# Six row tiles of the last product as seven block products over pairs of tiles, with the sums of w_out's blocks formed in the opening and kept in DRAM

## The chip, the core and the metric

The kernel runs on one core of a Trainium2 chip. The metric is the device time of one execution in microseconds; the median of three runs of the kernel before is 822.89 us (822.22 to 822.99). Times in the profile are counted from the start of the span.

## The reference, cut to what matters

One layer of a hybrid encoder block on x of 1024 rows by 1024 channels, float32. Everything up to `merged` stays as it is; the change touches the last product.

```python
h = rmsnorm(x, g_pre);  proj = h @ w_in
# stick-breaking attention (8 heads) and gated linear attention (4 heads), each gated and projected to 1024
merged = sigmoid(g_A) * y_sb + sigmoid(g_B) * y_gla
x = x + merged @ w_out                  # (1024 x 1024) @ (1024 x 1024): the last product
y = rmsnorm(x, g_final)
```

## The kernel before

**Products.** A float32 operand is split into a high part (type float32r, made by a copy on ScalarE) and a low part (operand minus high part, a subtraction on VectorE). A product is three passes on TensorE: high by high, high by low, low by high. One matmul takes a 128x128 stationary tile and 512 columns of the moving operand.

**Opening.** SyncE loads the rows of x and the first tiles of w_in; ScalarE and VectorE normalise the rows (`x_normed` counts tiles), TensorE turns them in rounds of four (`turn_x`), and ScalarE (`h_high`) and VectorE (`h_low`) evacuate each round as the two parts of h. TensorE interleaves the rounds with the first projection tiles (`first_tile`) and a low-rank product. ScalarE and VectorE then evacuate q, k and v halves (`stage`), split q and k of the first heads (`stack`), and SyncE copies them to the other 64 partitions (`twin`, SBUF to SBUF). The attention loop `pair` follows: in each of its steps TensorE makes scores, ScalarE takes two sigmoids of them (`sig_done`), and the scores of the next step wait for that. All DMAs of weights go out from SyncE in the order in which they are written, on one queue. POOL only sets constants here.

**Gates and the merge.** Seven gate tiles v = 0 to 6 are each computed as seven block products (`gate_block`, 12 matmuls each; `prod_done` counts them). After the last of them `merge_last` writes the last channel tile of the merged matrix, `mT[:, 0]` (channels on partitions, all 1024 rows as columns); `m_step` reaches 23 then.

**Last product** (L925 to L945). For each of eight row tiles t and both column halves e, TensorE accumulates 24 matmuls (8 channel tiles, 3 passes) into one of four PSUM banks (`ring4`). The stationary operand is the merged tile, split by `split_m` on ScalarE (L1326) and VectorE (L1837); tile 0 is split in two goes (`split_m0`, L1213 and L1741), since its last channel tile comes late. The moving operand is w_out, loaded by `load_wout` (L512) in eight chunks and split by `wout_high` and `wout_low`. The bank's order is t0 e0, t0 e1, t1 e0 and so on. VectorE adds x to each bank (`row_sum`, L1861), ScalarE sums the squares and takes the root, VectorE scales (L1875), SyncE stores. The last half row has a path of its own: L1346 (squares), L1350 (root), L1889 (reciprocal), L1891 and L1354 (scaling), L546 and L548 (stores). POOL spreads g_final over the partitions (L577).

## Time and profile before

| what | value |
|---|---|
| median of three runs | 822.89 us |
| the profiled execution's own time | 822.67 us |
| its span | 820.9 us |
| TensorE matmul busy | 799.9 us (97%) |
| VectorE busy | 551.0 us (67%) |
| ScalarE busy | 394.8 us (48%) |
| POOL busy | 10.6 us (1%) |
| DMA engines' mean busy share | 25.1% on the one large queue, 63.13 MB |

The page gives shares over the whole span; the order of work at a given place is read from the timeline, and what sets the end from the chain that ended last. The granted clock of TensorE is full in all 40 slices of the page. Matmuls overlap, so one that is listed with 389 ns occupies less than that of the chain.

### The profile page before, as it was taken

The page shows a single profiled execution, that of the slowest core. Times are in us where ns is not written, and L with a number is a line of the kernel's source. Part 1 is how long each engine was busy: PE and PEld are TensorE (multiplying, and loading weights), DVE is VectorE, ACT ScalarE, POOL GpSimd, SP SyncE. Part 2 cuts the span into 40 slices and gives each one's busy share as a digit, 9 for nine tenths or more (in the row PEclk, how much of TensorE's full clock was granted, in tenths as well). Part 3 has the DMA queues.
Part 4 walks back from the last instruction along what each step waited for, and adds up shares of the span by engine and source line. Part 5 has one row for each costly group of instructions (what it writes and reads, how often), then busy time and mean ns, then how long its engine had stood idle before and what let it go on. Part 6 is the DMA issues. An engine that isn't in the chain of part 4 may idle for free.

```text
span 820.9 us, 11756 instructions
## 1 busy us (share of the span) xinstructions
PE 799.9 (97%) x4477; PEld 669.1 (82%) x4477; DVE 551.0 (67%) x776; ACT 394.8 (48%) x679; POOL 10.6 (1%) x16
## 2 busy tenths in 40 slices
PE   5999999999999999999999999999999999999997
PEld 4778888888888888879889888888888888878885
DVE  6528896989698698946545655665467776873332
ACT  8536675756666465654254153344333333542221
POOL 1000000000000000020000000000000000010000
PEclk9999999999999999999999999999999999999999
DMA  8122011212110220121110001243433444352321
GB/s 290 54 52 52 26 40 40 49 43 59 38 39 26 52 51 26 27 78 53 52 32 21 28 27 52 89 148 131 144 104 104 121 126 127 138 206 102 103 101 54
DMA packets 69714, 63.72 MB, mean 78 GB/s; under 512 B 3724, under 2 KB 57127, under 8 KB 69672
## 3 DMA queue, kind: packets, MB, share of 16 engines
q1 hardware_dynamic: 69618, 63.13, 25.1%
q8 instruction: 29, 0.48, 0.2%
q14 instruction: 13, 0.11, 0.0%
q10 hardware_dynamic: 54, 0.01, 0.0%
HBM read 47.40 MB, written 11.53 MB: 72 GB/s over the span
## 4 chain that ended last, share of the span: by engine, by line
PE 82%; DVE 10%; issue 3%; ACT 2%; DMA 2%; DVEq 0%; SPq 0%; ACTq 0%
PE pj L611 21%; PE ob L942 5%; PE ob L863 5%; PE sc L863 5%; PE sc L942 5%; PE tr L915 4%; PE pj L755 4%; PE ob L915 4%; DVE surv L1460 4%; PE pj L627 4%; PE pj L915 4%; PE ob L703 3%; PE sc L915 3%; PE tr L713 3%; PE pj L736 3%
## 5 line engine op out<-in xcount | busy, mean ns | idle before, releaser
L611 PE MATMUL pj<-h_hi,w_lo 128*128 128x512 f32 x336 | 134.2, 399 | 0.0
L611 PE MATMUL pj<-h_hi,w_hi 128*128 128x512 f32 x336 | 133.8, 398 | 0.0
L611 PE MATMUL pj<-h_lo,w_hi 128*128 128x512 f32 x336 | 133.7, 398 | 0.0
L1460 DVE TENSOR_TENSOR_SCAN surv<-surv 128x128 f32<-128x128 f32 (+3 forms) x64 | 86.5, 1351 | 19.2 <-ACT beta L1046 18.7
L611 PEld LDWEIGHTS pj<-h_hi,w_lo 128*128 128x128 f32 x336 | 63.5, 189 | 12.1 <-issue 0.5
L611 PEld LDWEIGHTS pj<-h_lo,w_hi 128*128 128x128 f32 x336 | 63.3, 188 | 12.1 <-issue 0.3
L611 PEld LDWEIGHTS pj<-h_hi,w_hi 128*128 128x128 f32 x336 | 63.5, 189 | 11.7 <-issue 0.2
L1087 ACT ACTIVATE wt_hi<-tr 128x512 fp32r<-128x512 f32 (+2 forms) x96 | 43.6, 490 | 43.2 <-PE tr L713 41.7
L1385 DVE TENSOR_TENSOR w_lo<-w_raw,w_hi 128x1024 fp32r<-128x1024 f32 x33 | 40.3, 1222 | 26.6 <-ACT w_hi L980 26.5
L1505 DVE TENSOR_TENSOR wt_lo<-tr,wt_hi 128x512 fp32r<-128x512 f32 (+2 forms) x96 | 50.1, 549 | 5.3 <-ACT wt_hi L1087 4.8
L1463 DVE TENSOR_TENSOR beta<-beta,surv 128x128 f32<-128x128 f32 (+3 forms) x64 | 48.6, 759 | 2.2
L1045 ACT ACTIVATE surv<-sc 128x128 f32<-128x128 f32 (+3 forms) x64 | 41.8, 654 | 13.8 <-PE sc L681 13.0
L713 PE MATMUL tr<-ident,beta 128*128 128x128 f32 x288 | 43.1, 277 | 4.0 <-DVE wt_lo L1505 4.0
L1046 ACT ACTIVATE beta<-sc 128x128 f32<-128x128 f32 (+3 forms) x64 | 41.6, 651 | 0.0
L713 PEld LDWEIGHTS tr<-ident,beta 128*128 128x128 f32 x288 | 32.4, 140 | 11.1 <-DVE wt_lo L1505 5.9
L980 ACT ACTIVATE w_hi<-w_raw 128x1024 fp32r<-128x1024 f32 x33 | 34.9, 1057 | 9.7 <-PE ob L863 9.3
L703 PE MATMUL ob<-wt_hi,v_st 128*128 128x256 f32 (+1 forms) x160 | 38.0, 272 | 0.5
L703 PE MATMUL ob<-wt_lo,v_st 128*128 128x256 f32 (+1 forms) x160 | 37.6, 282 | 0.0
L679 PE MATMUL sc<-k_hi,q_st 128*128 128x512 f32 (+2 forms) x96 | 37.1, 387 | 0.0
L755 PE MATMUL pj<-vn_hi,h_hi 128*128 128x256 f32 x128 | 36.5, 285 | 0.1
L755 PE MATMUL pj<-vn_hi,h_lo 128*128 128x256 f32 x128 | 36.4, 284 | 0.0
L755 PE MATMUL pj<-vn_lo,h_hi 128*128 128x256 f32 x128 | 36.3, 284 | 0.0
(326 smaller groups left out, 1868.2 us busy)
## 6 DMA issues: line engine op xcount, KB each, us to landing
w_raw<-in_w_in SPq DMA_DIRECT2D x30, 512.0 KB, 3.8
y_scratch<-y_ring SPq DMA_DIRECT2D x28, 256.0 KB, 2.0
graw<-in_w_in SPq DMA_DIRECT2D x14, 512.0 KB, 4.7
y_back<-y_scratch SPq DMA_DIRECT2D x14, 512.0 KB, 5.2
x_t<-in_x SPq DMA_DIRECT2D x8, 512.0 KB, 6.4
wout_raw<-in_w_out SPq DMA_DIRECT2D x8, 512.0 KB, 7.0
x_res<-in_x SPq DMA_DIRECT2D x8, 512.0 KB, 3.7
out_y<-y_out SPq DMA_DIRECT2D x16, 256.0 KB, 2.2
```

The source lines that it names most:

```text
L611: mm = pe.matmul(pj[bank][:, :], (w_lo if p == 2 else w_hi)[:, slot, k, :], (h_lo if p == 1 else h_hi)[:, k, HALF * h:HALF * h + HALF], st ...
L703: mm = pe.matmul(ob[gg % 2][:, c0:256], v_st[:, e, b, :], part[g % 2][:, b, c0:256], start=(b == 0 and part is wt_hi), stop=(b == blocks - ...
L713: mm = pe.transpose(tr[n % 2][:, P * b:P * b + P], beta[:, unit % 2, P * (b0 + b):P * (b0 + b) + P], ident[:, :])
L755: mm = pe.matmul(pj[c % 2][:, 256 * (t % 2):256 * (t % 2) + 256], (h_lo if p == 2 else h_hi)[:, k, P * t:P * t + P], (vn_lo if p == 1 else ...
L863: mm = pe.matmul(ring4[c % 4], (w_lo if p == 2 else w_hi)[:, slot, 4 * side + k, :], (g_lo if p == 1 else g_hi)[:, G_SLOT[4 * br + k], HAL ...
L915: mm = pe.matmul(bank_of, (gw_lo if p == 2 else gw_hi)[j][:, k, :], moving[j][p == 1][:, k, :], start=(j < 4 and k == 0 and p == 0), stop= ...
L942: mm = pe.matmul(ring4[c % 4], (m_lo if p == 2 else m_hi)[t % 2][:, k, :], (wout_lo if p == 1 else wout_hi)[e][:, u, :], start=(u == 0 and ...
L1045: act.activation(surv[:, step % 2, 0:keys], sc[:, 0:keys], ACT.Sigmoid, scale=-HD ** -0.5)
L1087: act.activation(wt_hi[g % 2][:, b0:b0 + nb, P * (unit % 2):P * (unit % 2) + P], tr[n % 2][:, 0:P * nb].rearrange("p (b q) -> p b q", q=P) ...
L1460: dve.tensor_tensor_scan(s[:, ::-1], s[:, ::-1], s[:, ::-1], 1.0, ALU.mult, ALU.bypass)\
L1463: dve.tensor_tensor(beta[:, step % 2, 0:keys], beta[:, step % 2, 0:keys], surv[:, step % 2, 1:keys + 1], ALU.mult).then_inc(w_ready, 1)
L1505: dve.tensor_tensor(wt_lo[g % 2][:, b0:b0 + nb, qs], tr[n % 2][:, 0:P * nb].rearrange("p (b q) -> p b q", q=P), wt_hi[g % 2][:, b0:b0 + nb ...
```

## The change

Rows of x in tiles 0 and 1 are computed as before, in another order (both tiles by one column half, then both by the other). Tiles 2 to 7 are taken in three pairs p = 1, 2, 3. A pair's 256 rows by 1024 channels and w_out's 1024 by 1024 are each cut into four blocks, and the pair's result is made of seven block products (`out_block`) of 12 matmuls instead of eight. The four sums of w_out's blocks do not depend on the data: POOL forms them in the opening from w_out's rows, ScalarE and VectorE split them, and SyncE stores both parts in DRAM (`w_scratch`, eight stores of 1 MB) and reads them back (`load_tw`, eight loads of 1 MB) around the start of the last product. The sums of the merged blocks are formed by POOL per pair. VectorE puts the seven products together in nine steps (`gather`, counted by `pair_step`) on x_res, which now holds four rows of tiles; ScalarE copies one bank out per pair (`copy_u2`). y_row and y_out are gone: rows are scaled in place and stored whole, with one DMA for 512 KB, but for tile 6, the last, which is stored in halves. In the opening the eight small loads of w_up are issued later.

```diff
+        x_res = at("x_res", 8, [P, 4, D])
...
+        w_dram = nc.dram_tensor("w_scratch", (2, 4, P, 4, HALF), F32, kind="Internal").ap()
...
+            def load_wrow(k):
+
+                if k >= 2:
+                    sp.wait_ge(wsum_done, 4 * (k - 2) + 4)
+                sp.dma_start(wrow[k % 2][:, :, :], w_out_v[:, k::4, :]).then_inc(wrow_loaded[k % 2], 16)
+
+            def store_wsum(part, k):
+
+                if part == 0:
+                    sp.wait_ge(wsum_hi, 2 * k + 2)
+                else:
+                    sp.wait_ge(wsum_lo, 2 * k + 2)
+                sp.dma_start(w_dram[part, :, :, k, :].rearrange("t p c -> p t c"),
+                             (wsum_l if part else wsum_h)[k][:, :, :].bitcast(F32))\
+                    .then_inc(wsum_stored[4 if k == 3 and part else k], 16)
@@ -447,10 +489,23 @@
...
 
+            load_wrow(0)
+            load_wrow(1)
             load(3, COL_Z, 1)
             load(4, COL_Q + P, 0)
+            for c in range(8):
+                sp.dma_start(w_up[RANK * c:RANK * (c + 1), :], w_alpha_up[0]).then_inc(up_loaded, 16)
+            load_wrow(2)
+            load_wrow(3)
+            for k in range(3):
+                for part in range(2):
+                    store_wsum(part, k)
             twin(0, 2)
             load(5, COL_K + P, 1)
+            for part in range(2):
+                store_wsum(part, 3)
+            for n, stores in enumerate((32, 32, 32, 16, 16)):
+                sp.wait_ge(wsum_stored[n], stores)
@@ -525,29 +580,51 @@
...
+            def load_tw(n):
+
+                for part in range(2):
+                    sp.dma_start(tw[n][part][:, :, :].bitcast(F32), w_dram[part, n]).then_inc(tw_loaded[n], 16)
...
-                if t >= 2:
...
-                    store(t - 1)
+            sp.wait_ge(prod_done, NP * NP - 1)
+            load_tw(2)
+            sp.wait_ge(m_step, 3 * NP + 2)
+            load_res(0)
+            sp.wait_ge(prod_done, NP * NP)
+            load_tw(3)
+            sp.wait_ge(wout_l, KT)
+            load_tw(1)
+            sp.wait_ge(o5_ready, 2)
+            load_tw(0)
+            load_res(1)
@@ -561,6 +638,22 @@
...
+            pool.wait_ge(x_normed, ST)
+            for k in range(4):
+                top, low = wrow[k % 2][:, 0, :], wrow[k % 2][:, 1, :]
+                ts = wsum[k]
+                pool.wait_ge(wrow_loaded[k % 2], 16 * (k // 2) + 16)
+                if k == 2:
+                    pool.wait_ge(tr_ready, R0)
+                if k == 3:
+                    pool.wait_ge(wsum_stored[0], 32)
+                pool.tensor_tensor(ts[:, 0, :], top[:, HALF:D], top[:, 0:HALF], ALU.subtract).then_inc(wsum_done, 1)
+                pool.tensor_tensor(ts[:, 2, :], low[:, HALF:D], top[:, HALF:D], ALU.subtract).then_inc(wsum_done, 1)
+                pool.wait_ge(wsum_done, 4 * k + 1)
+                pool.tensor_tensor(ts[:, 1, :], low[:, HALF:D], ts[:, 0, :], ALU.subtract).then_inc(wsum_done, 1)
+                pool.wait_ge(wsum_done, 4 * k + 3)
+                pool.tensor_tensor(ts[:, 3, :], low[:, 0:HALF], ts[:, 1, :], ALU.subtract).then_inc(wsum_done, 1)
@@ -575,6 +668,24 @@
...
+
+            pool.wait_ge(m_ready, 2)
+            pool.wait_ge(m_step, 3 * NP + 2)
+            for p in range(1, 4):
+                a, b = slice(2 * P * p, 2 * P * p + P), slice(2 * P * p + P, 2 * P * p + 2 * P)
+                o11, o21, o12, o22 = mT[:, 4:KT, a], mT[:, 4:KT, b], mT[:, 0:4, a], mT[:, 0:4, b]
+                if p > 1:
+                    pool.wait_ge(om_low, NP * (p - 2) + 6)
+                pool.tensor_tensor(os3[:, :, :], o11, o21, ALU.subtract).then_inc(os_ready, 1)
+                pool.wait_ge(os_ready, 4 * (p - 1) + 1)
+                pool.tensor_tensor(o21, o21, o22, ALU.add).then_inc(os_ready, 1)
+                pool.wait_ge(os_ready, 4 * (p - 1) + 2)
+                if p == 1:
+                    pool.wait_ge(o5_ready, 4)
+                pool.tensor_tensor(os2[:, :, :], o21, o11, ALU.subtract).then_inc(os_ready, 1)
+                pool.wait_ge(os_ready, 4 * (p - 1) + 3)
+                pool.wait_ge(om_low, NP * (p - 1) + 1)
+                pool.tensor_tensor(o12, o12, os2[:, :, :], ALU.subtract).then_inc(os_ready, 1)
...
+            for c in range(4):
+                t, e, part = c % 2, 1 - c // 2, c // 2
+                if c == 0:
+                    pe.wait_ge(comb, 5 * (NP - 1))
+                    pe.wait_ge(sig_a, 2 * (NP - 1))
+                if c == 1:
+                    pe.wait_ge(mt_lo, 3)
...
+            READ_BY = {4: 3, 5: 2, 6: 4}
+            TW_OF = {1: 3, 3: 0, 4: 1, 5: 2}
...
+                if o in READ_BY:
+                    pe.wait_ge(pair_step, done + READ_BY[o])
+                if p == 1 and o in TW_OF:
+                    pe.wait_ge(tw_loaded[TW_OF[o]], 32)
+                pe.wait_ge(om_low, NP * (p - 1) + o + 1)
+                bank_of = gate_banks[(p + 1) % 2][OUT_BANK[o]]
+                for j in range(4):
+                    for q in range(3):
+                        mm = pe.matmul(bank_of, (om_lo if q == 2 else om_hi)[o][:, 3 - j, :],
+                                       out_moving[o][q == 1][:, j, :], start=(o < 4 and j == 0 and q == 0),
+                                       stop=(j == 3 and q == 2), skip_group_check=True)
@@ -1022,17 +1166,39 @@
...
+            def wsum_high(k, half):
+
+                hs = slice(2 * half, 2 * half + 2)
+                act.wait_ge(wsum_done, 4 * k + 4)
+                if k == 2:
+                    act.wait_ge(wsum_stored[0], 32)
+                act.activation(wsum_h[k][:, hs, :], wsum[k][:, hs, :], ACT.Copy).then_inc(wsum_hi, 1)
...
-            h_high(range(KT + 3, R0))
+            h_high([KT + 3])
+            wsum_high(0, 0)
+            h_high([KT + 4])
+            wsum_high(0, 1)
+            h_high(range(KT + 5, R0))
             stage(v_t, 2, 0, 0)
+            for half in range(2):
+                wsum_high(1, half)
             stage(stage_q, 3, 1, 1)
+            for half in range(2):
+                wsum_high(2, half)
             stage(stage_k, 4, 1, 0)
             act.wait_ge(proj_free, 5)
+            act.wait_ge(wsum_stored[1], 32)
             for part in range(2):
                 stack(0, part)
             high_part(3, 1, 2, proj_ready, 5)
+            wsum_high(3, 0)
             stage(v_t, 5, 1, 1)
+            wsum_high(3, 1)
             lr_quarters(1)
+            act.wait_ge(wsum_lo, 8)
+            act.wait_ge(wsum_stored[2], 32)
+            act.wait_ge(wsum_stored[3], 16)
 
@@ -1318,40 +1484,93 @@
...
+            def high_out(p, o):
+
+                if p == 1:
+                    if o < 3:
+                        act.wait_ge(prod_done, NP * NP)
+                        act.wait_ge(m_step, 3 * NP + 2)
+                    if o == 3:
+                        act.wait_ge(fin_bc, 1)
+                    if o >= 4:
+                        act.wait_ge(o5_ready, 4 if o == 6 else 3)
+                else:
+                    act.wait_ge(out_prod, NP * (p - 2) + o + 1)
+                if o >= 3:
+                    act.wait_ge(os_ready, 4 * (p - 1) + (2, 3, 1, 4)[o - 3])
+                act.activation(om_hi[o][:, :, :], out_source(p, o), ACT.Copy).then_inc(om_high, 1)
@@ -1437,16 +1656,37 @@
...
+            def wsum_low(k, half):
+
+                hs = slice(2 * half, 2 * half + 2)
+                dve.wait_ge(wsum_hi, 2 * k + half + 1)
+                dve.tensor_tensor(wsum_l[k][:, hs, :], wsum[k][:, hs, :], wsum_h[k][:, hs, :].bitcast(F32),
+                                  ALU.subtract).then_inc(wsum_lo, 1)
...
+            h_low(range(KT + 3, KT + 5))
+            wsum_low(0, 0)
+            h_low([KT + 5])
+            wsum_low(0, 1)
+            h_low(range(KT + 6, R0))
             stage(v_t, 2, 0, 0)
+            for half in range(2):
+                wsum_low(1, half)
             stage(stage_q, 3, 1, 1)
+            for half in range(2):
+                wsum_low(2, half)
             stage(stage_k, 4, 1, 0)
+            dve.wait_ge(wsum_stored[1], 32)
             for part in range(2):
                 stack(0, part, part)
             low_part(3, 1)
             stage(v_t, 5, 1, 1)
+            dve.wait_ge(proj_ready, 6)
+            for half in range(2):
+                wsum_low(3, half)
             lr_quarters(1)
+            dve.wait_ge(wsum_stored[2], 32)
+            dve.wait_ge(wsum_stored[3], 16)
             dve.wait_ge(const_done, 1)
@@ -1848,47 +2083,113 @@
...
+            dve.wait_ge(mt_hi, 3)
+            dve.tensor_tensor(m_lo[1][:, :, :], mT[:, :, P:2 * P], m_hi[1][:, :, :].bitcast(F32), ALU.subtract)\
+                .then_inc(mt_lo, 1)
             for c in range(5, KT):
                 wout_low(c)
+            dve.wait_ge(xr_loaded[0], 32)
+            row_sum(0)
+            for o in range(2):
+                low_out(1, o, o)
+            row_sum(1)
+            for o in range(2, 4):
+                low_out(1, o, o)
+            row_sum(2)
+            row_sum(3)
+            low_out(1, 4, 5)
+            low_out(1, 5, 4)
+            low_out(1, 6, 6)
...
+            norm_row(0, 0)
+            norm_row(1, 1)
+
+            for p in range(1, 4):
+                row, done = 2 * (p % 2), OP_STEPS * (p - 1)
+                banks = gate_banks[(p + 1) % 2]
...
+                if p > 1:
+                    norm_row(2 * p - 2, 2 * ((p - 1) % 2) + 1)
+                    norm_row(2 * p - 1, 2 * ((p - 1) % 2))
+                dve.wait_ge(xr_loaded[p % 2], 32 * (p // 2 + 1))
+                gather(1, 1, xa1, banks[0], xa1, ALU.add, 0)
+                gather(2, 2, xb2, xb2, banks[3], ALU.subtract, 0)
+                next_low(0)
+                next_low(1)
+                gather(3, 3, xa1, banks[1], xa1, ALU.add, 1)
+                next_low(2)
...
+                next_low(3)
+                dve.wait_ge(u2_copied, p)
+                gather(5, 5, xa2, o_sum[:, :], xa2, ALU.add, 0)
+                next_low(4)
+                gather(6, 6, o_sum[:, :], o_sum[:, :], banks[3], ALU.add, 5)
+                gather(6, 7, xb1, xb1, o_sum[:, :], ALU.add, 6)
+                gather(6, 8, xb2, xb2, o_sum[:, :], ALU.add, 6)
+                next_low(5)
+                gather(7, 9, xa2, banks[2], xa2, ALU.add, 5)
+                next_low(6)
+
+            dve.wait_ge(ss5, 15)
+            dve.wait_ge(y_done, 5)
+            dve.reciprocal(stats[:, 52:53], stats[:, 50:51]).then_inc(rstd5, 1)
+            dve.wait_ge(rstd5, ST - 1)
+            dve.scalar_tensor_tensor(out=x_res[:, 3, :], in0=x_res[:, 3, :], scalar=stats[:, 52:53], in1=g_fin[:, :],
+                                     op0=ALU.mult, op1=ALU.mult).then_inc(y_done, 1)
+            dve.wait_ge(ss5, 17)
+            dve.wait_ge(y_done, 6)
```

## Rows read from the trace of the kernel before

**Rows 1.** The page, section 1: busy time by engine (share of span, instructions).

```profile
PE 799.9 (97%) x4477; PEld 669.1 (82%) x4477; DVE 551.0 (67%) x776; ACT 394.8 (48%) x679; POOL 10.6 (1%) x16
```

**Rows 2.** Chain that ended last, last product: start us, us, what.

```profile
732.37 6.41 PE sc L942 x27
...
749.66 10.88 PE sc L942 x48
```

**Rows 3.** The same chain in the opening.

```profile
59.15 3.05 PE pj L611 x13
62.19 0.12 PE sc L679
```

**Rows 4.** Timeline of ScalarE, opening: start us, us, engine, line, operation, tiles, shapes.

```profile
50.68 1.06 ACT L991 ACTIVATE q_st<-stage_q 64x1024 fp32r<-64x1024 f32 x1 [0.49 <-DVE stage_k L1399]
...
59.33 1.28 ACT L1040 ACT_TABLE_LOAD   x1
...
60.89 0.27 ACT L1046 ACTIVATE beta<-sc 128x128 f32<-128x128 f32 x1
```

**Rows 5.** Timeline of VectorE, opening: the last row tile normalised.

```profile
24.80 0.75 DVE L1380 TENSOR_SCALAR x_t<-x_t,stats 128x1024 f32<-128x1024 f32 x1
```

**Rows 6.** Timeline of SyncE's queue: the first twin copy and the loads behind it.

```profile
54.27 0.54 SPq L439 DMA_DIRECT2D k_hi<-k_hi  x1
...
55.49 12.57 SPq L423 DMA_DIRECT2D w_raw<-in_w_in  x2
```

**Rows 7.** Windows: length, engines' busy time, PEclk, DMA share, GB/s at the end.

```profile
55.50:56.00 0.50, 0.50 (x4) 0.25 (x3) 0.34 (x1) 0.13 (x1) 0.00 (x0) 1.00 0.99 221
...
59.50:60.00 0.50, 0.50 (x4) 0.41 (x3) 0.26 (x1) 0.50 (x1) 0.00 (x0) 1.00 0.44 129
...
819.00:819.50 0.50, 0.00 (x0) 0.00 (x0) 0.00 (x0) 0.00 (x0) 0.00 (x0) 1.00 1.02 389
```

**Rows 8.** Timeline of POOL over the whole span.

```profile
14.58 0.28 POOL L559 TENSOR_SCALAR_AFFINE_SELECT ident_bf<-ident_bf 128x128 bf16<-128x128 bf16 x1 [11.68 <-issue]
...
361.28 0.68 POOL L570 TENSOR_SCALAR_AFFINE_SELECT mask<-mask 128x512 f32<-128x512 f32 x1
362.02 1.58 POOL L573 TENSOR_SCALAR_AFFINE_SELECT mask<-mask 64x512 f32<-64x512 f32 x1
...
726.92 2.23 POOL L577 PARTITION_BROADCAST g_fin<-g_fin_row  x1 [363.25 <-DMA g_fin_row<-in_g_final]
```

**Rows 9.** Timeline of ScalarE around and in the last product.

```profile
697.72 0.63 ACT L1254 ACTIVATE gw_hi<-graw 128x512 fp32r<-128x512 f32 x1 [5.08 <-DMA graw<-in_w_in]
...
731.68 0.31 ACT L1213 ACTIVATE m_hi<-mT 128x128 fp32r<-128x128 f32 x1 [2.35 <-DVE mT L1846]
731.90 2.00 ACT L1205 ACTIVATE wout_hi<-wout_raw 128x1024 fp32r<-128x1024 f32 x2
...
750.43 1.06 ACT L1335 ACTIVATE junk<-y_row 128x1024 f32<-128x1024 f32 x1 [7.17 <-DVE y_row L1861]
```

**Rows 10.** Timeline of VectorE around and in the last product.

```profile
728.49 1.06 DVE L1844 TENSOR_TENSOR gates<-gates,y_back 128x512 f32<-128x512 f32 x1
...
730.19 0.69 DVE L1844 TENSOR_TENSOR gates<-gates,y_back 128x512 f32<-128x512 f32 x1
...
732.02 0.29 DVE L1741 TENSOR_TENSOR m_lo<-mT,m_hi 128x128 fp32r<-128x128 f32 x1 [0.42 <-ACT m_hi L1213]
732.23 3.49 DVE L1749 TENSOR_TENSOR wout_lo<-wout_raw,wout_hi 128x1024 fp32r<-128x1024 f32 x3
735.64 1.22 DVE L1837 TENSOR_TENSOR m_lo<-mT,m_hi 128x1024 fp32r<-128x1024 f32 x1
...
742.53 1.42 DVE L1875 SCALAR_TENSOR_TENSOR y_out<-y_row,stats,g_fin 128x512 f32<-128x512 f32 x2
```

**Rows 11.** Timeline of all engines, the tail.

```profile
816.85 0.17 DVE L1889 RECIPROCAL stats<-stats 128x1 f32<-128x1 f32 x1 [1.18 <-ACT stats L1350]
...
818.17 0.43 SPq L548 DMA_DIRECT2D out_y<-y_out  x1
```

267 lines of the change are left out of this document (169 added, 98 removed).

## Prediction

> **What bounds the kernel now.** I read the engine line of the page first: TensorE is busy 97% of the span and no other engine over 67% [rows 1]. So an edit gains only if it takes matmuls away, and costs only where it makes TensorE wait. Next, the chain that ended last, for the last product: 48 matmuls, two banks, take 10.88 us [rows 2], so one costs 10.88/48 = 0.2267 us. In that chain all is TensorE but one gap: at 732.37 us it resumes with 27 matmuls, three of the first bank and 24 of the second. It had waited for the last channel tile of row tile 0, whose parts come from ScalarE at 731.68 and VectorE at 732.02 [rows 9, 10]. Last, the opening, in which the change puts a second stage of work: TensorE makes the scores of step 0, runs 13 projection matmuls from 59.15, and at 62.19 makes the scores of step 1 [rows 3]. These need step 0's sigmoids, which end at 60.89 + 0.27 = 61.16 [rows 4]. That is 1.0 us of slack, and it is where I expect the main cost.
>
> **What is removed.** Before, 16 banks of 24 are 384 matmuls. After, 4 banks of 24 and 3 pairs of 7 products of 12 are 96 + 252 = 348. 36 fewer at 0.2267 us is **-8.16 us**. Each of the new products is on TensorE's path back to back, in the same three-pass form, so I take the same pace.
>
> **The sums of w_out in the opening.** POOL may start when the last row tile is normalised, 24.80 + 0.75 = 25.55 [rows 5]. It makes four operations of 128x512 for each of four k, 16 in all. No row shows a two-input operation on POOL. The nearest are a selection of the same shape at 0.68 us and one on 64 partitions at 1.58 us [rows 8]; I take the middle, 1.13, and 1.2 from start to start with the semaphore. The Trainium skill (GPSIMD Engine Reference, Performance versus the Vector engine) gives 4497 ns for a float32 tensor_tensor of 2048 elements; a quarter is an estimate of 1.12 us, and the sum would be the same by it.
>
> k = 0 is then done at 30.4 and k = 1 at 35.2. ScalarE takes the first of them behind a round of h at about 32.3 and TensorE needs the rounds behind it only from about 41, so these ten copies and subtractions lie in idle time of both engines. What does not is SyncE's queue, since one DMA is served after the other. From k = 1 on it holds the load of rows k = 3 and six stores, 1 MB each. Stores run at 389 GB/s in the tail with the DMA engines full [rows 7]; with a little less, 380, one takes 2.76 us. The first is issued at 35.2 and starts 1.1 us later, as the twin copy issued at 54.27 does, which has the engines full by 55.5 [rows 6, 7]. So 36.3 + 7 x 2.76 = 55.6: the queue is never empty, and k = 1's stores land just at about 50.5, when ScalarE and VectorE, who now wait for them, would split q and k at 50.68 [rows 4]. The twin copies and the load of w_raw behind them hold the engines from about 55.3 to 59.8 before, 4.5 us [rows 6, 7]; now from 55.6 to 60.1. The store of k = 3's high parts is issued at about 56.7 (ScalarE copies them after the v half) and comes behind: 60.1 + 2.76, and 0.4 until its semaphore, 63.3. ScalarE and VectorE wait for exactly this store before the loop. Behind ScalarE's wait are a table load of 1.28 us and the first sigmoids, 61.16 - 59.33 = 1.83 us in all [rows 4]: 65.1 against the 62.19 at which TensorE needs them. The stall is **+3.0 us**. Its ends: if the store did not queue behind the copies it would land at 56.7 + 1.1 + 2.76 + 0.4 = 61.0 and the stall be 0.6; if a POOL operation takes 1.58, everything behind the eighth moves by 8 x 0.45 = 3.6 us, 6.6 in all. Afterwards nothing is given back, since TensorE is full from there.
>
> **The order of tiles 0 and 1.** Bank 1 is now tile 1, not tile 0, and waits for the whole low part of tile 1. ScalarE makes the high part after tile 0's last piece, at 731.90, in about 1.04 us (it did two of 1024 in 2.00), and VectorE the low part in 1.22 [rows 9, 10]: 731.90 + 1.04 + 0.04 + 1.22 = 734.20. TensorE ends bank 0 at 732.37 + 3 x 0.2267 = 733.05. **+1.2 us**; before, this work had a whole bank as cover. POOL now starts its first sum of the merged tiles at the same event as tile 0's last piece. The one row with POOL and VectorE busy together is a multiplication of 128x512 at 728.49, which takes 1.06 us under the broadcast that starts at 726.92 for 2.23; the same at 730.19 takes 0.69 [rows 8, 10]. I add this 0.37 once: **+1.6 us** in all. Ends 1.2 and 3.3 (the lock, below).
>
> **The first pair.** Its fifth product reads into a bank that VectorE must have gathered (step 3). Count from the end of bank 3. VectorE adds bank 3 (0.7), ScalarE sums and roots the row (1.5, from 1.06 and two small ones), copies a sum's high part (0.6), VectorE makes three low parts (1.85 at 0.6 from start to start), scales two rows (a reciprocal of 0.17 and 1.42 each, 3.2), gathers twice and makes two low parts (2.4), and gathers step 3 (0.7): 11.0 us [rows 9 to 11]. TensorE comes there after 48 matmuls, 10.88. So 0.1 to 0.3 us, and with 0.4 for POOL, which forms the second pair's sums in just this stretch, **+0.7 us**; ends 0.2 and 2.5. In pair 2 no row adds and fewer low parts come ahead of step 3, 8.4 against 10.9: covered. The loads of the sums are 8 MB. The last that the first pair needs early (fourth product, about 759) is issued at 739.7 behind about 4 MB, 11 us at 389 GB/s: on chip at about 753, covered by 6 us.
>
> **The tail.** The last half row's path is the same, but VectorE has a whole row to scale (1.42) and its reciprocal (0.17) between, after the row's root, about 0.9 us after TensorE ends. It is free at 2.5 us, while before the last reciprocal came 1.9 us after the end [rows 10, 11]: +0.6. That row's store of 512 KB is ahead of the last two, 1.35 us of the queue, most of it over before the last is issued 3.8 us after TensorE's end: +0.3. **+0.9 us**, ends 0.6 and 1.3. The x loads and stores of the pairs have over 5 us each.
>
> **The sum.** -8.16 + 3.0 + 1.6 + 0.7 + 0.9 = -1.96 us. The profiled execution takes 822.67 us, 0.2 under the median of 822.89; the same difference on the median gives 820.9 us.
>
> **Rivals.** (1) *The opening is nearly free*: the store of k = 3 does not queue behind the copies, stall 0.6, and the sum is -4.4, 818.5 us. For it: the copies between partitions move only 221 GB/s with the engines at 0.99 [rows 7], so something may run beside them. Against: the same 0.99. (2) *POOL is slow*, and the forecast turns to slower: the price is 8 times what an operation takes over 1.2 us from start to start. At 0.45 us more, the 1.58 of the row, the sum is -1.96 + 3.6 = +1.7 and with the first pair later by 0.8, +2.5: 825.4 us. It decides from 1.6 us per operation. A worse form: the first selection on POOL came 11.68 us late with nothing shown to wait for [rows 8]; such a start-up before the first sum would move the whole queue and give +9 and more. (3) *POOL and VectorE exclude each other* in the last product. If the first sum runs first, tile 0's last piece at 732.02 waits 0.9 us and tile 1's low part a second operation of 1.2, bank 1 starts 2.1 us later still than by the 1.2 above, 3.3; and in the first pair two scalings wait one POOL operation each, 2.5. Sum: -8.16 + 3.0 + 3.3 + 2.5 + 0.9 = +1.5, 824.4 us. Against: at 728.49 the operation ended at 729.55, though the broadcast ran to 729.15 and 0.69 more would be 729.84 [rows 8, 10]. By the Trainium skill (SBUF — State Buffer, "SBUF: two separate sides") a VectorE operation with two inputs in SBUF and a POOL operation that reads SBUF lock each other out for a whole instruction; the row agrees in sign and not in full size. (4) *The products don't come at the full pace*, because the sums arrive late: at the 221 GB/s of the copies the 6 MB and x ahead of the fourth product take 33 us from 733, 766 against 759, +7 and 828 us.
>
> **How the numbers follow.** Forecast 0.43 (819.3 to 822.6 from its own ends), rival 1 0.22, rival 2 0.17, rival 3 0.13, rival 4 0.05. About 0.2%, 1.65 us, is what a measurement of this kernel can tell from no change. Faster by more takes rival 1 and over half of the forecast, 0.46; within it the rest of the forecast and part of rival 3, 0.32; slower 0.22. The range takes in rivals 1 to 3 but the start-up: 817.6 to 825.6.
>
> **What would show it.** Steps: 348 matmuls in the last product at 10.88 us per 48; POOL's operations of 128x512 at 1.1 us, the first at 25.6; a wait of TensorE of 3 us for the first sigmoids at about 62, with ScalarE idle until the store of k = 3's high parts has landed; one of 1.6 us more at bank 1, ended by tile 1's low part; under 1 us at the fifth product of pair 1; 0.9 us more from TensorE's end to the span's. The prediction is wrong if the DMA engines are idle between 40 and 55 us, if POOL's operations take 1.6 us, or if VectorE's operations beside POOL's are stretched by a whole one.

## The result, and the profile after

The changed kernel takes 827.7 us (median of 8 runs, 826.3 to 831.3) where the kernel before, run beside it, takes 823.1. The ratio is 1.0063, with a 95% interval of 1.0045 to 1.0081: slower by 0.6%. The forecast was 820.9, faster, with a range of 817.6 to 825.6. The profiled execution took 827.49 us, and what follows is read from it; its span is 825.2, 4.3 more than the 820.9 before. Two slow executions, one of e3 below (2039 us) and one of the kernel before (921 us), are left out of all medians, ranges and ratios.

The page of the changed kernel, busy time by engine, beside [rows 1]:

```profile
PE 795.7 (96%) x4441; PEld 664.1 (80%) x4441; DVE 585.2 (71%) x807; ACT 410.1 (50%) x705; POOL 54.7 (7%) x44
```

There are 36 matmuls fewer, as said, and TensorE is busy 4.2 us less, not 8.2: part of its work ran at a lower clock, which lengthens busy time. Its waits come on top. The waits of TensorE in the changed kernel (instruction <- what ended the wait: us in total, times, longest):

```profile
PE sc L790 <- DMA k_lo<-k_lo: 2.4, 1, 2.4
...
PE sc L790 <- ACT beta L1212: 1.6, 1, 1.6
PE sc L1050 <- DVE m_lo L1981: 2.4, 1, 2.4
...
PE pj L1082 <- DVE x_res L2148: 1.3, 1, 1.3
PE sc L1050 <- DVE m_lo L2117: 0.9, 1, 0.9
```

Of these the kernel before has only one, 1.3 us for m_lo. The first two stand in the opening, the others in the last product. Its other waits differ by 0.2 us at most.

**The opening.** The chain of the changed kernel there (start us, us, what), which before was TensorE alone [rows 3]:

```profile
41.06 4.04 DVE wsum_l L1663 x2
...
45.12 7.53 DMA w_scratch<-wsum_l
...
52.73 1.07 ACT q_st L1135
...
53.90 1.97 DVE q_st L1626
...
58.36 0.60 SPq L450
...
59.00 7.18 DMA w_scratch<-wsum_h
...
68.08 0.18 ACT beta L1212
68.25 0.04 issue
68.30 0.38 PE sc L790
```

Read it upwards. The second row of scores starts at 68.30, because ScalarE could not begin the loop before k = 3's high store had landed (59.00 + 7.18). SyncE issued that store behind two twin copies and a load, and these behind the split of q and k, which waited until 52.7 for k = 1's low store. That store was issued at 45.12 and not earlier because VectorE took 4.04 us for two low parts that take 1.22 each when alone. By TensorE's timeline the same row started at 62.03 before: 6.3 us.

GpSimd's timeline (POOL in the profile) in the changed kernel (start us, us, line, operation, tiles, shapes, idle before):

```profile
25.71 1.29 POOL L650 TENSOR_TENSOR wsum<-wrow 128x512 f32<-128x512 f32 x1 [21.77 <-DVE x_t L1599]
...
41.74 2.27 POOL L653 TENSOR_TENSOR wsum<-wrow,wsum 128x512 f32<-128x512 f32 x1
44.09 2.15 POOL L655 TENSOR_TENSOR wsum<-wrow,wsum 128x512 f32<-128x512 f32 x1
...
733.51 1.30 POOL L670 PARTITION_BROADCAST g_fin<-g_fin_row  x1 [363.49 <-DMA g_fin_row<-in_g_final]
742.13 1.75 POOL L679 TENSOR_TENSOR os<-mT 128x512 f32<-128x512 f32 x1 [7.32 <-issue]
...
763.75 1.67 POOL L679 TENSOR_TENSOR os<-mT 128x512 f32<-128x512 f32 x1 [1.36 <-DVE om_lo L2102]
765.50 2.15 POOL L681 TENSOR_TENSOR mT<-mT 128x512 f32<-128x512 f32 x1
```

Alone an addition takes 1.29 us. Beside VectorE's low parts it takes 2.2, and the two low parts together grow by 1.7 (4.04 for 2.37, e4b below).

Windows of the changed kernel (length, TensorE busy, granted clock, DMA share, GB/s), beside [rows 7]:

```profile
55.50:56.00 0.50, 0.50 (x4) 1.00 1.05 410
...
62.00:63.00 1.00, 1.00 (x4) 0.50 1.04 275
63.00:64.00 1.00, 1.00 (x4) 0.50 1.09 409
```

At 55.5 the DMA engines are full with stores at 410 GB/s, where the twins' copies moved 221 before. From 62 to 65 the granted clock is 0.50, the 1.2 GHz level, behind the wait of 2.4 us for the twins' k_lo: by the timeline a matmul of the projection starts every 0.43 us, and every 0.23 us before.

**The last product.** Chain of the changed kernel, which answers to [rows 2, 9, 10]:

```profile
733.52 2.23 DVE mT L2069
...
739.31 1.05 ACT m_hi L1491
...
740.38 1.24 DVE m_lo L2117
741.62 0.04 issue
741.66 7.04 PE sc L1050 x24
...
764.38 2.12 DVE x_res L2112
...
771.13 0.61 DVE x_res L2148
771.75 0.04 issue
771.79 3.02 PE pj L1082 x12
```

The last merge of 1024 columns took 2.23 us beside the broadcast that started 0.01 us ahead of it (1.23 where it starts first, in the runs below); tile 1's low part ends at 741.62, 0.9 us after bank 0; and the 24 matmuls behind it take 7.04 us instead of 5.44. Of these 1.6 us, 0.3 is the restart behind a wait (f1 has the same 24 at a clock of 1.00 in 5.74) and 1.3 the clock, which is at 0.50 from 741.7 to 744. Further on two scalings of a row take 2.12 us each under GpSimd's sums. The products themselves run at 2.72 us per 12, the pace of [rows 2].

### The profile page after: what moved, and what is told of

It is laid out like the page before. It is cut to its first block, busy times and chain, and to the rows that moved or that the text cites. A ratio compares the mean times of both kernels' runs of the same rounds, so it can differ in the third digit from the quotient of the medians.

```text
span 825.2 us, 11846 instructions
## 1 busy us (share of the span) xinstructions
PE 795.7 (96%) x4441; PEld 664.1 (80%) x4441; DVE 585.2 (71%) x807; ACT 410.1 (50%) x705; POOL 54.7 (7%) x44
## 4 chain that ended last, share of the span: by engine, by line
PE 76%; DVE 12%; issue 4%; DMA 4%; ACT 3%; SPq 0%; DVEq 0%; ACTq 0%
PE pj L722 21%; PE ob L974 5%; PE sc L974 5%; PE tr L1026 4%; PE pj L866 4%; PE ob L1026 4%; DVE surv L1700 4%; PE pj L1026 4%; PE ob L814 3%; PE sc L1026 3%; PE tr L824 3%; PE pj L847 3%; PE pj L738 2%; PE sc L791 2%; PE sc L790 2%
## 5 line engine op out<-in xcount | busy, mean ns | idle before, releaser
L722 PEld LDWEIGHTS pj<-h_hi,w_lo 128*128 128x128 f32 x336 | 63.9, 190 | 12.3 <-issue 0.5
L1211 ACT ACTIVATE surv<-sc 128x128 f32<-128x128 f32 (+3 forms) x64 | 41.8, 653 | 13.1 <-PE sc L792 12.3
```

The costliest lines, as they stand in the source:

```text
L722: mm = pe.matmul(pj[bank][:, :], (w_lo if p == 2 else w_hi)[:, slot, k, :], (h_lo if p == 1 else h_hi)[:, k, HALF * h:HALF * h + HALF], st ...
L1211: act.activation(surv[:, step % 2, 0:keys], sc[:, 0:keys], ACT.Sigmoid, scale=-HD ** -0.5)
```

## The experiments

One number for each run is the ratio to the kernel before, timed in turns on the same chip. Since the opening alone varies from run to run, the profiled executions are also cut in two: the start of the second row of scores, and the rest of the span behind it. These two columns are of a single execution each, for f2 and h2 the slowest of the run (829.6 and 823.5 us), for f1 and h4 the second fastest (823.6 and 817.9). With the last product of the changed kernel as it is, e5, f1, f2 and f4 have a rest of 755.1 to 757.8, so a difference of 1 or 2 us in that column alone says little. The fences show only the lines of an edit that carry its idea.

| kernel | us, median (range) | ratio, 95% interval | second row | rest |
|---|---|---|---|---|
| before | 823.1 to 823.7, by set of runs | 1 | 62.0 | 758.9 |
| after | 827.7 (826.3 to 831.3) | 1.0063 [1.0045, 1.0081] | 68.3 | 756.9 |
| e1_opening_alone | 830.8 (829.7 to 831.9) | 1.0086 [1.0069, 1.0103] | 69.4 | 759.7 |
| e2_last_alone | 820.4 (819.3 to 821.3) | 0.9956 [0.9939, 0.9973] | 62.6 | 757.0 |
| e3_high_stores | 826.1 (824.7 to 827.8) | 1.0032 [1.0017, 1.0047] | | |
| e4b_no_pool | 832.7 (831.4 to 833.6) | 1.0107 [1.0090, 1.0124] | 75.8 | 755.6 |
| e5_short_sums | 825.5 (822.8 to 827.5) | 1.0029 [1.0017, 1.0041] | 65.8 | 757.8 |
| f1_stores_behind | 826.3 (822.7 to 828.3) | 1.0030 [1.0016, 1.0045] | 66.1 | 755.1 |
| f2_own_places | 825.4 (821.0 to 829.6) | 1.0017 [1.0001, 1.0033] | 70.3 | 756.8 |
| f3_twins_first | 827.8 (826.2 to 830.7) | 1.0047 [1.0028, 1.0066] | 64.5 | 763.2 |
| f4_places_again | 824.4 (819.6 to 826.3) | 1.0001 [0.9984, 1.0017] | 66.1 | 756.1 |
| g1_broadcast | 828.0 (825.5 to 830.6) | 1.0055 [1.0038, 1.0073] | 69.7 | 756.8 |
| g2_tile_order | 824.9 (824.1 to 827.4) | 1.0027 [1.0008, 1.0047] | 68.4 | 753.4 |
| g3_sums_later | 824.9 (823.6 to 829.4) | 1.0030 [1.0016, 1.0045] | 68.4 | 754.6 |
| g4_last_mended | 829.3 (826.6 to 829.6) | 1.0055 [1.0035, 1.0076] | 69.0 | 758.5 |
| g5_no_broadcast | 823.4 (822.7 to 824.4) | 0.9994 [0.9982, 1.0006] | 69.6 | 752.7 |
| h2_all | 820.3 (818.9 to 823.5) | 0.9965 [0.9953, 0.9977] | 67.1 | 754.3 |
| h3_all | 828.9 (828.2 to 829.5) | 1.0057 [1.0044, 1.0071] | 64.6 | 763.1 |
| h4_all | 820.1 (816.3 to 821.5) | 0.9953 [0.9935, 0.9971] | 64.1 | 751.8 |

**Which half costs: e1, e2.** Each has one half of the change.

```
e1:  the sums, their stores and waits in the opening; the last product of the kernel before
e2:  w_dram filled with pieces of h once h is free; pairs' products, loads and tail of the change
```

> The kernel before with the opening of the change alone: the sums of w_out's blocks are formed, split and stored in DRAM, the last product is the old one and never reads them. Theory A (the loss comes from the opening, where TensorE's scores of step 1 came 6.1 us late in the changed kernel): about 829.2 us, 6.1 over the 823.1 before, with the same gap in TensorE at 59 to 68 us. Rival B (the opening's stall is given back later, and the last product is what loses): 824 us or less.

> The last product of the change alone, with the opening of before: no sums are formed; w_scratch is filled instead with eight 1 MB pieces of h around 430 us, when the queue is idle, and read back as the operands (the sums are left out, so the output is not the reference's). Theory A: the changed kernel less its opening, 827.7 - 6.1 = 821.6 us, that is 36 matmuls gained (8.2 us) and about 6.6 given back at tiles 0 and 1, the first pair and the tail. Rival B: 823 us or more.

Against the 823.6 of the kernel before in the same set, the opening alone costs 7.2 us and the last product alone gains 3.2. That is +4.0 together, and the change has +4.6: the halves add to within their spread.

**Traffic or order: e3.** Only the high parts are stored, and loaded twice.

```
-                for part in range(2):
-                    store_wsum(part, k)
+                store_wsum(0, k)
```

> The changed kernel with only the four stores of high parts; the low parts are formed but not stored, and the loads of low parts read the high ones (output not the reference's). It halves the bytes that the opening writes, and keeps POOL's work. Theory C (the queue's backlog makes the opening's stall): no wait at the split of q and k, the copies to the other partitions land at about 59.5, the last store at about 62, stall about 2.5 us instead of 6.1: 824.1 us. Rival D (POOL and VectorE shutting each other out makes it): the subtractions of 2.0 us stay and the time is within 1 us of 827.7.

Half of the stores' traffic is gone and 1.6 us with it, between the two theories. The wait for the last high store is still in the code, so the run does not settle it. No profile of it is shown.

**GpSimd's share: e4b, e5.**

```
e4b: ScalarE and VectorE split w_out's own rows; GpSimd's sixteen additions left out
e5:
-                pool.tensor_tensor(ts[:, 0, :], top[:, HALF:D], top[:, 0:HALF], ALU.subtract)
+                pool.tensor_tensor(ts[:, 0, 0:16], top[:, HALF:HALF + 16], top[:, 0:16], ALU.subtract)
```

> The changed kernel without GpSimd's sums: ScalarE and VectorE split w_out's own rows instead, and GpSimd has no instruction between the masks and the attention's end. The high and low parts that are stored are those of w_out's rows and not of the sums, so row tiles 2 to 7 come out of other blocks; loads, copies, subtractions, stores and waits are otherwise those of the changed kernel. Theory C (the opening's stall of 6.1 us is at least a third due to GpSimd and VectorE shutting each other out: VectorE's low parts at 2.0 to 4.0 us instead of 1.2, which delays the store that the stack of the first heads' q and k waits for): VectorE's low parts fall to about 1.25 us, the first pair's second row of scores comes about 2 to 3 us sooner, 824.7 to 825.7. Theory D (the stall is set by the queue of 1 MB stores and SyncE's order, GpSimd has no part in it): the low parts fall too, but the last high store still lands at about 66, within 0.7 of 827.7.

> The changed kernel with GpSimd's sixteen additions of the opening cut to 16 columns each, and two memsets of the sums' places at its start; copies, low parts, loads, stores and waits stay. What is stored is not the sums of w_out's blocks (the rest of each piece is what lies in its place), so row tiles 2 to 7 come out of other blocks. Theory C, sized anew after the run without GpSimd was spoilt by its own loads (the port's share of the opening's 6.1 us): VectorE's low parts at 1.2 us each instead of 2.0 to 2.3, the first q_st part at 0.97 instead of 1.97, the second low store issued 1 to 2 us sooner, hence the second row of scores 2 us sooner, 825.7 (825.0 to 826.3). Theory D (the queue of the stores alone): the second low store lands at 52.5 to 53 as before, the last high store at 66, within 0.5 of 827.7.

e4b did not measure what it was made for. Its loads of w_out's rows waited for VectorE instead of GpSimd, and SyncE could issue the first four stores only behind them, from 44.4 on. Its chain:

```profile
41.53 2.37 DVE wsum_l L1652 x2
...
46.38 15.02 DMA w_scratch<-wsum_l
```

The two low parts take 2.37 us without GpSimd, against 4.04. And the store lands 15 us after issue, with four transfers of its size ahead, which shows how the opening hangs on the store's place in the queue: the stall grew by 7.5 us. e5 keeps the loads and makes the additions short. Its timeline of VectorE:

```profile
41.11 2.36 DVE L1669 TENSOR_TENSOR wsum_l<-wsum,wsum_h 128x1024 fp32r<-128x1024 f32 x2
...
52.12 1.22 DVE L1632 TENSOR_TENSOR q_st<-stage_q,q_st 64x1024 fp32r<-64x1024 f32 x1 [1.20 <-ACT q_st L1141]
```

The second row comes 2.5 us sooner and the time falls by 2.2, as theory C said. The short additions also have the sums ready sooner, which would be a rival. But the low parts of k = 1 start at the same place as in the changed kernel (41.11 and 41.06) and end 1.7 us sooner, and the low part of q takes 1.22 instead of 1.97: these two account for 2.4 of the 2.5.

**The stores' waits: f1, f2, f3, f4.** All four move the sums' places so that waits for stores fall away or come later.

```
f1:
-            act.wait_ge(wsum_stored[1], 32)      # ahead of the stack
-            act.wait_ge(wsum_stored[3], 16)      # ahead of the loop; wsum_h3 at 92 instead of 108
f2:  as f1, and wsum_h1 at F + 28 and F + 44, wsum_h2 at 104
-                if k == 2:
-                    act.wait_ge(wsum_stored[0], 32)
f3, f4:  as f2, and
-            for k in range(3):                   # stores of k = 0, 1 stay ahead of the twins
+            for k in range(2):
                 for part in range(2):
                     store_wsum(part, k)
             twin(0, 2)
             load(5, COL_K + P, 1)
+            for k in range(2, 4):  ...
f3:  wsum_l3 at 100 and 120 (z_sig's place)     f4:  wsum_l3 at 100, wsum_h2 at 112
```

> The changed kernel with two waits of the opening taken away by other places: the stack of q and k waits only for the second high store (a semaphore of its own), whose 8 KB k_lo takes, and the second low store is waited for only before the loop; the fourth high part goes to w_v's place at 92 KB, split once the sixth bank is done, and its store is waited for only before the first write of G. Theory A (the opening's 6.1 us are these two waits, 2.0 at the stack and about 4 before the loop, and not the sums' own work): the stack is split at about 50.9 to 51.5 as before the change, ScalarE waits for no store before the loop, the second row of scores starts at 63 to 64, so 827.7 - 4.5 = 823.2 (822.2 to 824.2). Theory E (stores and engines are so full between 42 and 57 that the twins' copies and the loads land late anyway): TensorE waits 3 us or more for the twins' k_lo, the second row starts at 65.5 or later, 825.5 to 827.

> The changed kernel with every wait for a store taken out of the opening but one: the second high part in the later places of q_st1 and k_lo1 (two stores of half the size), the third where w_out's rows lay, the fourth in w_v's place; their stores are waited for where those places are first written in the loop, and SyncE waits for none until the tables are read back. Theory A (the opening's stall is the waits for stores: 2.0 us at the stack, 4 before the loop): the stack is split at 51 or earlier, the twins are copied by 59, TensorE's second row of scores starts at 62.5 to 63.5, 827.7 - 5.4 = 822.3 (821.6 to 823.3). Theory E (the queue of 1 MB transfers holds the twins' copies): the stack is early but TensorE waits 2 us or more for k_lo, and a lower clock behind that wait costs up to 1.6 more: 824.5 to 826.

> The kernel with the stores' own places, and in SyncE's order the twins' copies and the load of w_in's sixth piece ahead of the third and fourth pieces' stores (the fourth low part in two halves at 100 and 120 KB, so that VectorE waits for no store). Theory A (what is left of the opening's stall is the place of the twins in the queue of 1 MB stores): the twins land within 4 us of their issue instead of 6.4, TensorE waits under 1 us for k_lo and its clock stays at 1.0, the second row of scores starts at 62 to 63.5, 827.7 - 5.5 = 822.2 (821.2 to 823.2). Theory J (the engines' queue is full at 54 whatever SyncE's order, from the first two pieces' stores and the loads): the twins land after 6 us still, 824.5 to 825.8.

> The kernel with the twins first, and w_out's rows, the third high part and the fourth low part in other places again (112, 112 and 100 KB): every store has until its place's first write in the loop, the earliest 8 us behind the first row of scores. Theory A (the opening's stall was waits for stores, each of them avoidable by a place): no wait of 4 us at the gate, the second row of scores at 64 to 64.5, TensorE's waits in the loop as before the change: 827.7 - 4.0 = 823.7 (822.7 to 824.7). Theory L (the queue of 8 MB of stores, full until 72 or so, holds some other load or store of the first pair): a wait of 2 us or more in the first pair, 825.5 to 828.

f1 gained 1.4 us of the 4.5 that theory A expected. Without the wait before the loop the row started at 66.1 and no earlier: ScalarE had waited for k = 0's low store (8.6 us to land), the twins' copies came at 61.0, TensorE had stood 2.7 us, and its next 13 matmuls took 4.63 us instead of 3.05 [rows 3]. f2 shows a second one. Its chain:

```profile
55.09 2.21 DVE k_lo L1637
...
57.91 6.42 DMA k_lo<-k_lo
```

256 KB land 6.42 us after issue, behind 1 MB stores, as theory E had it; at that issue the engines move 422 GB/s. h2, with the same opening, has 6.4 too. This was not f1's trouble nor the changed kernel's: there the split came so late that the engines had run nearly empty (25 GB/s at 57.0 in f1), and the copies landed in 3.7 us, with the same six stores ahead of them. With the twins ahead of the later stores it is 3.69 us in f3 and f4, and in f3 the row starts at 64.5. But f3 lost 4.2 us soon after, where ScalarE needed the place of the fourth low store, which landed at 74.3, and the clock fell to 0.50 behind that wait. f4 puts that store's source where it is waited for only ahead of the first write of G, and no wait shows there. Its chain:

```profile
52.42 2.02 DVE q_st L1635
...
54.48 2.21 DVE k_lo L1638
...
57.28 3.69 DMA k_lo<-k_lo
...
61.09 0.32 PE sc L800
...
61.60 4.63 PE pj L732 x13
66.23 0.12 PE sc L800
```

Its median is 3.3 us under the change, within what theory A said (4.0). The row was to start at 64 to 64.5, and starts at 66.1 in this execution, since the clock fell behind the twins. What is left of the opening is again the two engines' meeting: the low parts of q and k, 1.22 us each in e4b, take 2.02 and 2.21 beside GpSimd's last additions, and TensorE waits 1.8 us for the copies of k behind them. No run moved that.

**Tiles 0 and 1: g1, g2.**

```
g1:
             pool.wait_ge(fin_loaded, 16)
+            pool.wait_ge(m_step, 3 * NP + 2)
             pool.partition_broadcast(...)
g2:
-                t, e, part = c % 2, 1 - c // 2, c // 2
+                t, part = c // 2, c % 2
     (tile 1's parts behind wout_low 5 to 7; load_tw(0) behind three banks)
```

> The changed kernel with one wait added: GpSimd's broadcast of g_final waits for the last merge (m_step 23). Theory A (the merge's last addition took 2.23 us instead of 1.23 because GpSimd's 1.30 us broadcast began 0.01 us before it and had the port): the addition is back at 1.23, tile 0's low part 1 us sooner, 827.7 - 1.0 = 826.7, and up to 1.6 less again if TensorE's clock does not fall at the shorter gap. Theory F (the addition is long for another reason, or the gain is eaten by the next wait): within 0.3 of 827.7.

> The changed kernel with tiles 0 and 1 taken in the order of the kernel before: tile 0's halves, then tile 1's, with m_hi and m_lo of tile 1 made behind wout's fifth to seventh parts, the table wt at 92 and 28 KB loaded when three of the four banks are done. Theory A (1.2 us wait at the second bank for tile 1's low part, and another 1.6 us because the granted clock fell to 0.5 behind that wait): no wait at the second bank, 24 matmuls at 5.44 us, 827.7 - 1.2 - 1.6 = 824.9 (824.5 to 826.5, the upper end if the first wait, for tile 0's low part, alone pulls the clock down). Theory G (the late load of the fourth table's pieces, 9.2 us from issue to landing behind the third bank, now reaches the fourth product): TensorE waits up to 1 us at the fourth product and the gain is under 2.

g1 gained nothing, and VectorE's timeline tells why:

```profile
735.43 1.23 DVE L2070 TENSOR_TENSOR mT<-gates,y_back 128x1024 f32<-128x1024 f32 x1 [0.33 <-ACT gates L1482]
...
740.33 1.11 DVE L1982 TENSOR_TENSOR m_lo<-mT,m_hi 128x128 fp32r<-128x128 f32 x1 [0.42 <-ACT m_hi L1380]
```

The merge is at 1.23 us, and now m_lo, 0.29 in [rows 10], lies beside the broadcast and takes 1.11. The same lock moved 5 us down the path. g2 gained 2.8 us, as theory A said: its chain has 27 matmuls behind a single wait of 1.4 us, at a granted clock of 1.00.

```profile
738.88 6.44 PE sc L1050 x27
```

Part of that is not its edit. The merge took 1.22 us in g2 too, and GpSimd's timeline has the broadcast long instead:

```profile
733.38 2.27 POOL L670 PARTITION_BROADCAST g_fin<-g_fin_row  x1 [363.28 <-DMA g_fin_row<-in_g_final]
```

Which of the two is long hangs on hundredths of a microsecond. The merge is at 1.22 or 1.23 where it starts first (e2, e4b, f1, f3, f4, g2, g3), at 2.2 where the broadcast is 0.01 or 0.02 us ahead (the changed kernel, f2), and at 1.64 where it is 0.6 ahead (e5).

**The first pair: g3.**

```
                     pool.wait_ge(om_low, NP * (p - 2) + 6)
+                    pool.wait_ge(pair_step, OP_STEPS * (p - 2) + 3)
```

> The changed kernel with one wait added: GpSimd's sums for the next pair wait for the third step of the pair before (pair_step 3, 12), so that they no longer lie beside the two scalings of the rows behind them. Theory A (the first pair's 1.6 us are the two scalings at 2.12 us instead of 1.28 beside GpSimd's sums, ahead of the third step): the scalings are at 1.28 us, the third step is gathered at most 0.3 us after the bank is free, TensorE waits 0 to 0.4 us there and its next 12 matmuls are at 2.72, 827.7 - 1.5 = 826.2 (825.8 to 826.8). Theory H (the scalings were late for their squares and not for their length, or the sums now come too late for the next pair's operands): the wait at step 3 stays over 0.9, or a new one stands at the second pair, within 0.5 of 827.7.

The scalings take 1.28 us each, TensorE does not wait at the fifth product, and its chain through the pair is unbroken. The rest of the span is 2.3 us shorter (1.5 expected); in this execution the merge too was at 1.22, so part of it is luck with the broadcast.

**Together, and the start-up: h2, g4, h3, g5, h4.**

```
g4:  g2 + g3, and     pool.wait_ge(o5_ready, 1)   ahead of the broadcast
g5:  g2 + g3, and
-            pool.partition_broadcast(g_fin[:, :], g_fin_row[0:1, :], P).then_inc(fin_bc, 1)
+            sp.dma_start(g_fin[:, :], g_final.partition_broadcast(P)).then_inc(fin_bc, 16)
     with GpSimd's first sum behind o5_ready 1
h2:  f2 + g1 + g2 + g3      h3:  f3 + g4      h4:  f4 + g5
```

> Four edits together on the changed kernel: the stores' own places in the opening, tiles 0 and 1 in the order of the kernel before, the broadcast behind the last merge, the pairs' sums behind the third step. Theory A (the terms add: -5.4, -2.8, 0, -1.5): 827.7 - 9.7 = 818.0 (817.0 to 819.5), which is before 823.2 less 8.2 for the 36 products, plus 0.9 for the tail and some 2 for what is left of the opening and of the first pair. Theory I (the store's traffic of 8 MB and the lower clock behind TensorE's short gaps come back elsewhere): 820 to 822.5.

> The changed kernel with three edits in its last product and its opening left alone: tiles 0 and 1 in the order of the kernel before, GpSimd's broadcast and sums behind the first bank (o5_ready 1), the next pairs' sums behind the third step. Theory A (the 3.6 us at tiles 0 and 1 are GpSimd's port on the path of the merge and of the low part, the second tile's low part, and the lower clock behind the longer gap): the last merge at 1.23 us, m_lo at 0.30, TensorE's gap 1.3 us as before the change, granted clock 1.0 behind it, x27 in 6.4 us, no wait at the third step: 827.7 - 3.6 - 1.5 = 822.6 (821.8 to 823.6). Theory K (the clock falls or the gap is long for the traffic of the tables and not for GpSimd): x27 in over 7 us, 824 to 825.

> Both together: the opening with its own places and the twins first, and the last product mended. Theory A (the terms add): 827.7 - 5.5 - 5.1 = 817.1 (816.0 to 818.5). If theory J or K holds instead of A: 819 to 820.5.

> The changed kernel with tiles 0 and 1 in the order of the kernel before, g_final spread over the partitions by a DMA of 512 KB instead of GpSimd's broadcast, and GpSimd's sums behind the first bank and, for the next pairs, behind the third step; the opening as in the changed kernel. Theory A (3.6 us at tiles 0 and 1 and 1.5 at the first pair are GpSimd's port, the order and the clock; what took it back in the run before was the start-up of the first addition behind the broadcast): first addition within 1 us of the first bank, m_lo 0.30, gap 1.1 to 1.4 us, clock 1.0, no wait at the pairs over 0.3: 827.7 - 5.1 = 822.6 (821.6 to 823.6). Theory M (the start-up comes with the first addition after any long pause of GpSimd): the sums are late again, 826 or more.

> Both together. Theory A (the terms add): 827.7 - 4.0 - 5.1 = 818.6 (817.0 to 820.0), faster than the kernel before by 0.5 to 0.8%. Under theories L or M: 821 to 825.

h2 takes f2's opening with g1 to g3. It missed theory A's 818.0 and came out at 820.3, in theory I's range: m_lo lay under the broadcast again (1.11 us), TensorE waited 2.2 us for it, and its next 27 matmuls took 7.99 us at the lower clock. g4 mended tile 0 (m_lo at 0.29, TensorE's wait 1.1 us, granted clock 1.00 behind it) and lost more than it won, 829.3 us where 822.6 was expected. GpSimd's timeline:

```profile
740.52 2.19 POOL L671 PARTITION_BROADCAST g_fin<-g_fin_row  x1 [369.74 <-PE sc L1052]
755.01 1.28 POOL L681 TENSOR_TENSOR os<-mT 128x512 f32<-128x512 f32 x1 [12.30 <-issue]
```

12.3 us pass between the broadcast and the next addition, with nothing shown to wait for. The sums were late, and TensorE stood 3.7 us in the first pair. h3 inherited this and f3's stall, and has 828.9 us where 817.1 was expected. g5 has no broadcast, and its first addition comes at once after a pause as long:

```profile
741.43 2.25 POOL L678 TENSOR_TENSOR os<-mT 128x512 f32<-128x512 f32 x1 [370.12 <-PE sc L1049]
```

So the start-up belongs to the addition behind the broadcast and not to the pause; h4, without a broadcast, has none either. g5 came to 823.4 us, within the range of theory A. Its rest is 752.7, and that of h4, with both halves mended, 751.8. Before less 8.2 for the products plus 0.9 for the tail is 758.9 - 7.3 = 751.6: in the last product of this execution little but the tail is left of the cost. (Tile 1's low part lies under GpSimd's first sum there, 2.31 us, and TensorE waits 0.3 for it; for m_lo it waits 0.8 where it waited 1.3 before.) h4 beats the kernel before by 0.5% (0.3 to 0.65%), and its median, 820.1, is 7.6 us under the change and just above theory A's range. The profiled execution is 2.2 us faster than the median; what the others lost was not seen, and a fall of the clock behind the twins, as f4 has it in the same opening, would be 1.6 of it. Its chain in the opening:

```profile
56.91 3.69 DMA k_lo<-k_lo
...
61.22 3.04 PE pj L731 x13
64.27 0.12 PE sc L799
```

## Why the prediction was wrong, step by step

**-8.16 for 36 matmuls: right.** 348 matmuls, 2.72 us per 12, and the rest of h4's profiled execution within 0.2 us of the sum.

**+3.0 for the opening: mis-sized, it was 6.3** (7.2 alone). The mechanism was as told: a full queue of stores, and k = 3's high store before the loop. Three links were short. (1) GpSimd's operation took 1.29 us and not 1.13, which by itself is within the ends (1.28 from start to start, for 1.2); but beside it VectorE's low parts took 2.0 instead of 1.22, and its own additions 2.2. So k = 1's low store was issued at 45.1 and landed at 52.7, and the stack waited 2 us where I had it "just" in time. That GpSimd and VectorE shut each other out I had as a rival, and priced it in the last product alone. e5 shows it in the opening: 2.5 us of the row and 2.2 of the time, and the two lengthened places of VectorE are 2.4 of that. (2) I had the queue of the DMA engines full up to the twins. It had run nearly empty at 57.5 us (25 GB/s); what held the last high store was the late split, and SyncE's order. It came behind the twins and the load there: ready at about 57.9, issued at 59.0, so that each late step moved all behind it; it took 7.2 us to land from 59.0, where I had 6.6 from 56.7. (3) TensorE's wait for the twins I did not have at all, nor the lower clock behind it, which here lay under the longer wait for ScalarE and came to the surface in f1 and f4 (4.63 us for 13 matmuls).

**+1.6 for tiles 0 and 1: mis-sized, it was 3.6.** Tile 1's low part cost 0.9 of the 1.2 forecast. The 0.37 for GpSimd was 1.0: in the row that I took it from, the operation met only the end of the broadcast; here the broadcast was first, by 0.01 us, which is luck, and befell two of the ten profiled executions that have the broadcast where the change has it. The other 1.6 us are the restart behind a second wait, 0.3, and the granted clock, 1.3, which I had as 1.0 throughout. g2 took away the order (2.8 us, with the clock and a luckier merge), g5 the broadcast.

**+0.7 for the first pair: mis-sized, 1.6.** The two scalings lay under GpSimd's sums in full, 0.84 us each (2.12 for 1.28), where I had added 0.4; g3 shows that this is all of it. It is within the ends.

**+0.9 for the tail: right.** TensorE's end to the span's end is 6.9 us against 6.0.

**The sum with the measured terms.** -8.2 + 6.3 + 3.6 + 1.6 + 0.9 = +4.2 us, and the spans differ by 4.3.

**The rivals.** Rival 3 was the true one in kind, and too small for being kept to one place. It had 824.4 us with 3.3 for tiles 0 and 1 and 2.5 for the first pair; with the opening's 6.3 for 3.0 it would have given 827.7. Its rule in the Trainium skill (SBUF — State Buffer, "SBUF: two separate sides") says that whichever starts first holds the shared port for its whole instruction, and the other blocks. The runs agree, less some 0.3 us: 0.29 to 1.11 for m_lo and 1.23 to 2.23 for the merge beside a broadcast of 1.30. I had weighed the rule against one row in which the overlap was partial, and let that row reduce it. Worked out with the 0.3 it agrees in full: from 728.49 to 729.15, 0.66 us of the broadcast were left, and the operation lost 0.37. And the kernel before had a second such meeting in its timeline of VectorE, the other way round:

```profile
726.75 1.23 DVE L1829 TENSOR_TENSOR mT<-gates,y_back 128x1024 f32<-128x1024 f32 x1 [0.34 <-ACT gates L1315]
```

This merge started 0.17 us ahead of the broadcast [rows 8] and kept its length; the broadcast took 2.23 us, and 1.30 where it is first. Rival 2's decision point was put at 1.6 us per operation; by its own price the sum turns at 1.96/8 over 1.2, 1.45 from start to start. Alone the additions stayed under both, at 1.28, and passed them only beside VectorE's work. Its start-up was real too, not ahead of the first sum but behind the broadcast. Rival 1 fell: k = 3's high store landed 7.2 us after its issue, and not the 4.3 that this rival had for a store with nothing ahead. Rival 4 fell: no product waited for a table.

The sign was wrong because three shares went the same way. Worked out as independent, 3.0, 1.6 and 0.7 had room for errors either way; in fact the lock between GpSimd and VectorE was in all three, with 2.4 us in the opening, 1.0 at tile 0 and 1.7 in the first pair, where the forecast had 0.37 and 0.4. The clock added 1.3.

## What to carry to other kernels

Work given to an idle GpSimd is not free while VectorE works with two operands from SBUF: price every such meeting at a whole instruction on whichever comes second, and look for it on every path to the bound engine. A buffer that is read by a store belongs where nothing is written until the queue ahead of that store is empty; other places and another order of the stores brought the second row from 68.3 to 64.1 here. And small copies on the path go ahead of the megabytes in the queue that issues them, where that queue is full when they come: 3.7 us for 6.4.
